# Four edits in a hybrid encoder step on one core: order of the first norm, slot pairs for keys and queries, layout of the stored u, a third chunk of 360 columns

## The reference

```python
h = rms_norm(x, g_norm1) * (1 + sc1) + sh1            # sh1, sc1, ... = silu(c) @ w_ada + b_ada
a_in, b_in, q, k, v, qi, ki, wi, gl = split_cols(h @ w_in)
a = a_in[..., :D] * sigmoid(a_in[..., D:])            # branch A: GLU, causal conv of 31 taps
y_a = silu(layer_norm(causal_dwconv(a))) @ w_pa
z = gelu(b_in); u = z[..., :D]                        # branch B: u * spatial gate of 8 groups
vg = layer_norm(z[..., D:])
y_b = (u * spatial_gate(vg, w_s, b_s, L)) @ w_pb
q = rms_norm(q per head) ; k = rms_norm(k per head)   # branch C: top-k keys by an indexer
o = sparse_attention(q, k, v, qi, ki, wi, ...)        # GQA softmax with ALiBi
y_c = o @ w_pc
m = gates[0] * y_a + gates[1] * y_b + gates[2] * y_c  # gates = sigmoid(gl)
x = x + g1 * (m @ w_o)
h2 = rms_norm(x, g_norm2) * (1 + sc2) + sh2
x = x + g2 * (square(relu(h2 @ w_1 + b_1)) @ w_2 + b_2)
```

## Time and profile before

| what | value |
|---|---|
| median of 3 runs | 2591.36 us (2590.98 to 2593.56) |
| the profiled execution, its own time | 2593.5 us |
| its span, first to last instruction | 2591.2 us |
| PE busy | 2424.1 us, 94% |
| DVE, ACT, POOL busy | 48%, 28%, 45% |
| mean granted TensorE clock | 0.971 of full |
| chain that ended last, by engine | PE 74%, issue 11%, DVE 5%, POOL 4%, ACT 3%, DMA 2% |

### The profile page before, as it was taken

One profiled execution on the slowest core, in us unless ns is written; L12 is line 12 of the kernel. 1 busy time (PEld: TensorE's weight loads), 2 busy tenths in 40 slices (PEclk: granted clock), 3 DMA queues, 4 the chain that ended last, 5 costly groups with the idle time before them and its releaser, 6 DMA issues.

```text
span 2591.2 us, 35623 instructions
## 1 busy us (share of the span) xinstructions
PE 2424.1 (94%) x13638; PEld 2219.1 (86%) x13638; DVE 1241.1 (48%) x2173; ACT 719.1 (28%) x940; POOL 1170.7 (45%) x583
## 2 busy tenths in 40 slices
PE   4889999999999999877899999996999999999999
PEld 3758999999977899743448999995999999999988
DVE  3269999999993333136672383114312112122212
ACT  3242232544333535535451211014100110110110
POOL 2411232888766411112223576556554454454452
PEclk9889999999999999989999999998999999999999
DMA  8012333322245312370004575510111111111012
GB/s 302 20 39 72 110 110 97 101 92 93 85 155 171 98 42 95 100 177 25 17 4 137 188 230 163 187 41 25 33 50 49 32 49 51 34 46 55 28 45 86
DMA packets 252503, 228.97 MB, mean 88 GB/s; under 512 B 13208, under 2 KB 223234, under 8 KB 252155
## 3 DMA queue, kind: packets, MB, share of 16 engines
q1 hardware_dynamic: 198528, 135.48, 17.6%
q10 hardware_dynamic: 53883, 92.29, 10.7%
HBM read 174.44 MB, written 53.30 MB: 88 GB/s over the span
## 4 chain that ended last, share of the span: by engine, by line
PE 74%; issue 11%; DVE 5%; POOL 4%; ACT 3%; DMA 2%; ACTq 0%; POOLq 0%; DVEq 0%
PE acc L1887 60%; PE acc L2057 7%; PE acc L2190 2%; POOL wlo L652 1%; DVE mx L1687 1%; PE acc L2165 1%; PE acc L1899 1%; DVE st L1683 1%; DVE probs L1683 1%; DMA st<-in_w_dw_dram 1%; DMA x1T<-xT_d 1%; PE acc L1948 0%; POOL wlo L666 0%; PE aux L2177 0%; DVE xa L1669 0%
## 5 line engine op out<-in xcount | busy, mean ns | idle before, releaser
L1887 PE MATMUL acc<-xa,whi 128*128 128x364 f32 x3408 | 853.2, 332 | 1.4 <-DVE xa L1669 0.9
L1887 PEld LDWEIGHTS acc<-xa,whi 128*128 128x128 f32 x3408 | 608.3, 190 | 10.1 <-issue 6.7
L1887 PE MATMUL acc<-xa,wlo 128*128 128x364 f32 x1704 | 563.1, 330 | 0.0
L1887 PE MATMUL acc<-xb,whi 128*128 128x364 f32 x2160 | 534.6, 329 | 3.2 <-POOL wlo L615 3.2
L612 POOL TENSOR_TENSOR whi<-raw,one 128x512 fp32r<-128x512 f32 (+2 forms) x133 | 205.8, 1547 | 418.6 <-PE acc L1887 363.8
L1887 PE MATMUL acc<-xf,whi 128*128 128x364 f32 x1536 | 381.7, 330 | 6.3 <-issue 6.3
L1887 PEld LDWEIGHTS acc<-xb,whi 128*128 128x128 f32 x2160 | 382.6, 188 | 3.5 <-POOL wlo L615 3.5
L1887 PE MATMUL acc<-xb,wlo 128*128 128x364 f32 x1080 | 354.8, 328 | 0.0
L1887 PEld LDWEIGHTS acc<-xa,wlo 128*128 128x128 f32 x1704 | 323.0, 190 | 0.0
L666 POOL TENSOR_TENSOR wlo<-raw,whi 128x1024 fp32r<-128x1024 f32 x68 | 165.2, 2430 | 293.1 <-ACT whi L929 234.6
L1887 PEld LDWEIGHTS acc<-xf,whi 128*128 128x128 f32 x1536 | 273.9, 189 | 6.6 <-issue 6.6
(11 more groups left out here) (318 smaller groups left out, 2874.7 us busy)
## 6 DMA issues: line engine op xcount, KB each, us to landing
raw<-in_w_in_dram SPq DMA_DIRECT2D x88, 512.0 KB, 3.8
wmod<-in_w_ada_dram SPq DMA_DIRECT2D x32, 512.0 KB, 4.4
raw<-in_w_dram SPq DMA_DIRECT2D x32, 512.0 KB, 3.9
raw<-in_w_dram SPq DMA_DIRECT2D x64, 256.0 KB, 2.7
gate_d<-st ACTq DMA_DIRECT2D x24, 546.0 KB, 2.8
st<-gate_d ACTq DMA_DIRECT2D x24, 546.0 KB, 4.9
m_d<-st ACTq DMA_DIRECT2D x16, 546.0 KB, 3.5
st<-m_d ACTq DMA_DIRECT2D x16, 546.0 KB, 5.4
```

The source lines that it names most:

```text
L1887: last = nc.tensor.matmul(acc[0:m, s, c, 0:CW], w[:, s, k, 0:m], x[:, half, k, CW * c:CW * (c + 1)], start=(k == 0 and p == 0), stop=(k == ...
```

## The change

1. First norm: PE does conditioning 0, 1 and 2 ahead of k = 0, and conditioning 3 after k = 1. ACT's and DVE's orders stay.
2. Keys and queries: tile and squares lie in slots (0, 1) and (2, 3) of `st` in turn, and logarithm and exponential are written over the squares. `qk_tile` is cut in `qk_out` (round, copy, square) and `qk_root` (logarithm, exponential); ACT does `qk_out` of a tile and then `qk_root` of the tile before it. PE's order stays.
3. u is stored as `u_d[group, token in its tile, tile x channel]`: stores are in pieces of 128 columns (512 bytes), a load is one row of 4096 bytes for each partition. y goes back to slots 0, 1 and 4 of `st` in turn (the last two groups to a place of their own), and to DRAM in one DMA of 1088 columns for each group; DVE waits with group g from 3 on for the store of group g - 3, and no longer for the transposes of g - 2.
4. All matmuls over chunks take 360 columns for the third chunk (`width(c)`), and the 4 columns behind it are zeroed once (one memset on DVE at the start).

Some semaphores are merged (`hist_tr` into `ws_tr`, `tl_st` into `out_dma`) with the same things waited for.

```diff
@@ helpers
+        def width(c):
+            return min(CW, TOK - CW * c)
...
         def y_place(g):
-            return st[:, g % 2, :]
+            return st[:, (0, 1, 4)[g % 3], :]
+        def y_out(g):
+            return y_place(g)[:, 0:TOK] if g < KT - 2 else y_last[:, g - (KT - 2), 0:TOK]
+        def pair_of(parity):
+            return stage(2 * parity), stage(2 * parity + 1)
@@ ACT, token_group
-                        act.dma_start(u_d[t, 0:c, 512 * half:512 * (half + 1)], u_place(k)[0:c]).then_inc(u_st[k % 4], 16)
+                        act.dma_start(u_d[TU * half:TU * (half + 1), 0:c, P * t:P * (t + 1)].rearrange("g p c -> p g c"),
+                                      flat(u_place(k)[0:c], P)).then_inc(u_st[k % 4], 16)
@@ ACT, keys and queries
-            def qk_tile(n, s, idx):
+            def qk_out(n, s, idx, parity):
+                line, squares = pair_of(parity)
                 act.wait_ge(prod, n + 1)
                 round_next(n, s)
-                wait(act, qk_ok, idx)
+                wait(act, qk_ok, idx - 1)
...
+            def qk_root(idx, parity):
+                _, squares = pair_of(parity)
                 for c in range(CH):
                     act.wait_ge(qk_mm, CH * idx + (c + 1))
...
             with act.Fori(1, H // 2) as i:
                 for j in range(2):
-                    qk_tile(2 * i + (N_Q + j), (N_Q + j) % 2, 2 * i + (NKV + j))
-                    query_out(i, j)
+                    qk_out(2 * i + (N_Q + j), (N_Q + j) % 2, 2 * i + (NKV + j), j)
+                    qk_root(2 * i + (NKV + j - 1), 1 - j)
+                    query_out(i, j - 1)
@@ ACT, mix
-                act.dma_start(flat(u_back(g)[:, 0:SEQ], P), u_d[0:TT, :, P * g:P * (g + 1)].rearrange("t p c -> p t c"))\
+                act.dma_start(u_back(g)[:, 0:SEQ], u_d[g, :, 0:SEQ]).then_inc(u_ld[g % 2], 16)
...
-                act.dma_start(flat(yb_d[g, :, 0:SEQ], P), cols).then_inc(yb_st, 16)
-                act.dma_start(yb_d[g, :, SEQ:TOK], vt[:, TT, P * g:P * g + DEC]).then_inc(yb_st, 16)
+                act.dma_start(yb_d[g, :, 0:TOK], y_out(g)).then_inc(y_sem(g), 16)
@@ DVE, mix
-                wait(dve, yt_tr, g - 1)
+                if g >= 3:
+                    dve.wait_ge(yb_st[g % 3], 16 * (g // 3))
@@ PE, gemm (and two more like it)
-                            last = nc.tensor.matmul(acc[0:m, s, c, 0:CW], w[:, s, k, 0:m],
-                                                    x[:, half, k, CW * c:CW * (c + 1)],
+                            last = nc.tensor.matmul(acc[0:m, s, c, 0:width(c)], w[:, s, k, 0:m],
+                                                    x[:, half, k, CW * c:CW * c + width(c)],
@@ PE, first norm
             conditioning(0)
             conditioning(1)
+            conditioning(2)
             for k in range(KT):
...
-                if k in (1, 3):
-                    conditioning(k // 2 + 2)
+                if k == 1:
+                    conditioning(3)
```

More of the change, by code:

```diff
@@ L325, in hybrid_stream_step @@
         vg_ok = sem("vg_ok")
-        mix_mm, yb_ok, yt_tr, yt_ev, yb_st = (sem(n) for n in ("mix_mm", "yb_ok", "yt_tr", "yt_ev", "yb_st"))
+        mix_mm, yb_ok, yt_tr, yt_ev = (sem(n) for n in ("mix_mm", "yb_ok", "yt_tr", "yt_ev"))
+        yb_st = [sem(f"yb_st{j}") for j in range(3)]
         xa_ok = sem("xa_ok")
@@ L1034, in _ @@
             root_of_tokens(1, 0, 4)()
-            def qk_tile(n, s, idx):
+            def qk_out(n, s, idx, parity):
+                line, squares = pair_of(parity)
                 act.wait_ge(prod, n + 1)
                 round_next(n, s)
-                wait(act, qk_ok, idx)
-                nc.scalar.activation(chunks(stage(0)), product(s), ACT.Copy)
-                nc.scalar.activation(chunks(stage(1)), product(s), ACT.Square).then_inc(ev_act, 1)
+                wait(act, qk_ok, idx - 1)
+                nc.scalar.activation(chunks(line), product(s), ACT.Copy)
+                nc.scalar.activation(chunks(squares), product(s), ACT.Square).then_inc(ev_act, 1)
+            def qk_root(idx, parity):
+                _, squares = pair_of(parity)
                 for c in range(CH):
                     act.wait_ge(qk_mm, CH * idx + (c + 1))
-                    nc.scalar.activation(st[:, 2, CW * c:CW * (c + 1)], aux[:, c % 2, 0:CW], ACT.Ln,
+                    nc.scalar.activation(squares[:, CW * c:CW * (c + 1)], aux[:, c % 2, 0:CW], ACT.Ln,
                                          bias=eps[:, 0:1]).then_inc(qk_rt, 1)
                 act.wait_ge(qk_rt, CH * idx + CH)
-                nc.scalar.activation(stage(3), stage(2), ACT.Exp, scale=-0.5).then_inc(qk_ri, 1)
-            act.wait_ge(tl_st, 48)
+                nc.scalar.activation(squares, squares, ACT.Exp, scale=-0.5).then_inc(qk_ri, 1)
+            act.wait_ge(out_dma, 16 * 5)
             for j in range(NKV):
@@ L1064, in query_out, with values_out @@
                 act.dma_start(q_d[bass.ds(2 * i + j, 1)].rearrange("a p n -> p (a n)"), stage(4)).then_inc(q_st, 16)
+            def values_out():
+                act.dma_start(new_v_p[0, 0].rearrange("(t p) n d -> p t (n d)", p=P), vtok[:, 0:TT, :]).then_inc(out_dma, 16)
+                act.dma_start(new_v_s[0, 0].rearrange("j n d -> j (n d)"), vtok[0:DEC, TT + 1, :]).then_inc(out_dma, 16)
             act.wait_ge(vg_ok, TT + 1)
-            for j in range(NKV):
-                qk_tile(N_KV + NKV + j, (N_KV + NKV + j) % 2, j)
+            qk_out(N_KV + NKV, (N_KV + NKV) % 2, 0, 0)
@@ L1206, in branch_pair @@
                         nc.scalar.activation(xb[:, 0, bass.ds(2 * i + j, 1), :], st[:, 4:5, 0:NT], ACT.Copy).then_inc(m_hi, 1)
+            for k in range(3):
+                act.wait_ge(yb_st[k], (32, 32, 64)[k])
             act.wait_ge(o_lo, len(ATT))
@@ L1294, in step @@
                 own.settle()
+            own.mark(nc.vector.memset(acc[:, :, CH - 1, TOK - CW * (CH - 1):CW], 0.0))
             own.mark(nc.vector.memset(s_acc[:, :], 0))
@@ L1656, in _ @@
             dve.wait_ge(yt_tr, KT)
+            for k in range(2):
+                dve.wait_ge(yb_st[k], 32)
             def one_over_sum(i):
@@ L2020, in _ @@
                                            ident[0:HIST, 0:HIST])
-            last.then_inc(hist_tr, 1)
+            last.then_inc(ws_tr, 1)
             def glu_pair(i, first=False):
```

84 lines of the change are left out of this document (44 added, 40 removed).

## The result

The changed kernel takes 2610.0 us (median of 4 runs, 2609.5 to 2610.7) against 2592.35 for the kernel before (4 runs): 17.7 us slower, a ratio of 1.0068 with a 95% interval of [1.0051, 1.0086]. The forecast was 2602, +10.5.

The account below looks back on a forecast made before the run. PE was taken to bound the kernel, mostly by the pace of its matmuls. Terms -6.5 - 10.5 + 24.0 + 10.5 - 7.0 = +10.5 on 2591.4 gave 2602 us; own range 2595 to 2610, whole range 2588 to 2615.

Parts of the forecast that it names:

- third chunk: Matmuls over chunks: 360 instead of 364 columns shorten 3552 matmuls at 0.446 to 0.458 ns a column, -6.5 us.
- first norm: Start of the kernel: conditioning 2 ahead of k = 0 lets ACT's later rows start earlier, -10.5 us.
- keys and queries, stall: Head means: the logarithm waits behind ACT's rounding, copy, square and table load, so PE's third chunk comes later, +24.0 us.
- the clock behind it: Keys and queries: PE's clock falls behind idle gaps of about 4.4 us and slows the next matmuls, +10.5 us.
- mix: Mix: seven groups take 3.8 us each instead of 4.77 as u and y move at the long-row rate, -7.0 us.
- What the end gives back: Behind the last query: the 6.16 us wait for ACT's square goes, some other waits come, 3.7 us back.
- A clock of 0.50 was granted for 3.10 us: Profile row behind 6.34 us of idleness: 10 matmuls ran slowly, taken as a loss of 1.4 us a stall.
- 3.21 held, 4.67 did not: PE's clock: full rate behind 3.21 us of idleness, slower behind 4.67, so 4.4 was taken to make it fall.
- The forecast's upper bound: Clock term in keys and queries: at most +19 us, if the low stretches last twice as long.
- The rival in which the clock holds: Keys and queries: the clock stays up over 4.4 us gaps, so 2591.4 us, no slower than before; chance 0.15.
- the bound of 11.25: First norm: row 4 starts 11.25 us earlier and all of it reaches the end, the largest gain allowed.

Follow-up runs that it names:

- the old order: The changed kernel with ACT's earlier order for keys and queries (copy and square, then logarithm and exponential of the same tile), slot pairs kept: 2569.5 us, ratio 0.9919.
- the layout kernel: The kernel before with u by group, y in three places, one store for y and the merged semaphores alone: 2585.8 us, ratio 0.9981.

## Why the prediction came out as it did

The direction and the cause were right, the size was 7 us short. In the traces keys and queries with their clock were 8.9 us worse than forecast, and the total is off by only 5.3 (+15.8 against +10.5) because 3.3 us in the attention, for which nothing was forecast, went the other way. So the total is nearer than its terms, and in part by luck. Term by term:

| term | forecast | alone, by ratio | in the traces |
|---|---|---|---|
| third chunk | -6.5 | -8.3 [-11.4, -5.2] | MLP -3.8, where 1.8 ns a matmul make -2.8 |
| first norm | -10.5 | -13.5 [-16.8, -10.1] | -11.3 at its end |
| keys and queries, stall | +24.0: 27.7 before the last query's end, -3.7 behind it | | +27.7 before that end |
| the clock behind it | +10.5: 9.1 before that end, 1.4 behind it | | +17.0 before that end |
| both together | +34.5 | +36.0 [32.4, 39.9] | +44.7 - 1.3 = +43.4 |
| mix | -7.0 | -4.9 [-7.8, -2.3] | -5.6, of which 3.2 are PE's idle time |

- **Keys and queries.** Right to 0.03 us at the third chunk (5.22 against 5.19), and to 0.1 in the sum of stalls. What the end gives back was put at 3.7, or 2.3 with its low clock, and is 1.3 in the traces (1.7 of PE's idle time). The kernel with the old order shows that the place of the logarithm is the whole of it, not the pairs.
- **The clock** is the term that was mis-sized: 9.1 forecast and 17.0 measured behind the same eight waits. "A clock of 0.50 was granted for 3.10 us" was one row, taken for all, and it was the rest of a low that had begun at least 3.6 us earlier, in the idle time; behind the new stalls the low stretches fell on up to 6.2 us of work (20 matmuls instead of 10). And "3.21 held, 4.67 did not" was read as a boundary; gaps of 3.43 and of 2.03 were followed by lows, one of 3.56 was not. So that the clock would fall behind 4.4 us was right, but the reason given (4.4 is nearer to 4.67) was not a sound one. The forecast's upper bound (+19, lows twice as long) held it. The rival in which the clock holds is out: filling PE's gap gave back 19.2 us.
- **First norm.** The rows came within 0.3 us of the forecast, and the gain was more than the bound of 11.25 that was called "all of it": the first products end at 87.0 to 91.2 us in the six traces with the new order and at 99.8 to 103.2 in the eight without, 12.9 apart in the mean. A part is clock, which the term left out: of the 11.3 in the two traces above, PE's idle time has 7.6 and its busy time 3.7 (clock 0.96 instead of 0.90).
- **Columns.** They paid in full, somewhat more than forecast. 4 columns were worth 2.5 ns a third-chunk matmul in the MLP (3.8 us over 1536), of which 1.9 lie in the third chunks (166.7 to 164.8 ns); the 364-column matmuls also came closer, 166.7 to 166.4, which is the rest. Why they did is open.
- **Mix.** The size was near (seven groups, by the starts of their transposes, took 27.3 us where 26.5 were forecast), the reason wrong and the size in part luck: the term was computed from u's and y's bytes alike at the rate of long rows, while nearly all of the gain in waiting stands in y's stores, and it is 3 to 4 us; the rest is the clock of the kernel before in this stage. In the changed kernel each of DVE's last six waits in the mix ends with a load of u, none with a store of y, so its new wait cost nothing.
- **The table load.** The Trainium skill (ScalarE: Activation LUTs, "What ACT_TABLE_LOAD costs") adds a drain of 1.38 us to a table load of 1.28. In the changed kernel the square ends at 1079.79, the load starts at 1079.81 and takes 1.28, and the logarithm starts at 1081.10, 0.01 behind it. The trace agrees with the load and disagrees with the drain: the stall has no room for one.

The attention is 3.3 us shorter in the changed kernel and within 0.1 in the layout kernel, which has the only edit near it; it was 2.4 longer with the pairs alone and 1.1 with the norm alone. Its windows, first before, then changed, then with the pairs alone:

```profile
1150.63:1372.96 222.33, 186.85 (x664) 100.76 (x664) 148.82 (x344) 112.41 (x237) 58.17 (x36) 0.92 0.09 21
1176.09:1395.08 218.99, 183.43 (x664) 99.38 (x664) 149.14 (x344) 112.33 (x237) 58.26 (x36) 0.94 0.08 21
1190.57:1415.33 224.76, 189.83 (x665) 102.98 (x665) 149.12 (x344) 112.40 (x237) 58.15 (x36) 0.90 0.08 21
```

PE's idle time is the same within 0.7 us (35.5, 35.6, 34.9), and the lengths follow the clock (0.92, 0.94, 0.90). So the 3.3 us are clock and not work. Why the clock came out so in each kernel stays open.

## What to carry to other kernels

Ahead of a reordering, write down for each wait of the busiest engine what now stands between the event and its release on the engine waited for: here it was 4 us of rounding, copies and table load that could wait, in front of a logarithm of half a us for each chunk that PE needed at once. Double buffers (the slot pairs) were sound; they paid only once the urgent piece went first and the rest behind it. A stall on TensorE costs more than its length: here 27.7 us of idle time brought 17.0 of slow matmuls, and work to throw away in the gap gave that part back. And where traces of two kernels are compared stage by stage, split each difference into idle and busy time of the busiest engine: a difference in busy time for the same instructions is clock, and in this kernel it came to 3 or 4 us in stages that no edit touched.

## What the runs showed of the hardware

- Behind equal gaps of 4.4 us in one kernel PE worked at the lower clock for 2.9 to 6.2 us; gaps of 2.03 to 3.56 went either way.
- A low clock can begin within the idle time (at least 3.6 us ahead of the matmuls in the kernel before, at most 0.8 in the changed one at 1081.72), so the slow matmuls seen behind a gap can be only the rest of a longer low.
- 24 throw-away matmuls in each of seven waits kept the clock at 0.98 over a stage where it was 0.85; the two waits left unfilled, 2.02 and 1.96 us, were each followed by a stretch at 0.50.
- In the mix, storing y as whole rows instead of 512-byte pieces took 10 us of the queues' 36 us of busy time, loading u as whole rows instead of 512-byte pieces 1 us, and y's whole rows made u's loads land sooner as well (3.5 us instead of 4.2).
- A matmul's spacing follows its columns from 328 to 512 at about 0.45 ns each (150.5, 164.8, 166.7, 232.7 ns at 328, 360, 364, 512).
- A load of the activation table took 1.28 us, and the next activation started 0.01 us behind it.
